# Two small moves in a decoder trunk kernel: one weight slot's high part ahead of an exponential, and a parameter transposition behind half of the query slots

## The chip, the cores and the metric

The kernel runs on one core of a Trainium2 chip. The metric is the device time of one execution in microseconds (us), as the median of three runs. TensorE is called PE here, VectorE is DVE, ScalarE is ACT, GpSimd is POOL and SyncE is SP. A line such as L725 is line 725 of the kernel file.

## What is computed

Two decoder layers over 256 tokens of width 1024, all in float32. Each layer projects the normalised tokens into queries, keys, values and two halves of a convolution module, runs windowed attention beside the convolution, projects back, and adds a feed-forward network: dense SwiGLU in layer 0, a mixture of eight experts (two per token) in layer 1.

```python
for layer in range(2):
    h = rms_norm(x, attn_norm_g[layer])
    proj = h @ w_in[layer]                      # q | k | v | conv value | conv gate
    q, k = rms_norm(q, q_norm_g[layer]), rms_norm(k, k_norm_g[layer])
    attn_out = sliding_window_attention(q, k, v, sinks[layer])
    conv_out = conformer_conv(value, gate, conv_w[layer], conv_b[layer], conv_ln_g[layer], conv_ln_b[layer])
    x = x + concat(attn_out, conv_out) @ w_out[layer]
    h = rms_norm(x, ffn_norm_g[layer])
    if layer == 0:
        x = x + (silu(h @ w_gate) * (h @ w_up)) @ w_down
    else:                                       # top 2 of 8 experts, weights from a softmax over the two
        for e in range(8):
            x = x + combine[:, e] * ((silu(h @ w_gate[e]) * (h @ w_up[e])) @ w_down[e])
```

## The kernel before

**Weight slots.** All weights stream through one sequence of slots of 128 x 2048 float32 (1 MB each). SP loads a slot into one of six `raw` buffers. ACT rounds it to `w_high` (function `high`, L725), DVE computes `w_low` = raw minus high (function `low`, L1034), and PE multiplies every tile three times: high by high, high by low, low by high (function `terms`). `w_high` and `w_low` have three buffers each, so `high(s)` waits for three things: that slot s has landed, that PE has finished slot s-3 (semaphore `w_used`), and its own place in ACT's program. `low(s)` waits for `high(s)`, and PE's function `slot(s, ...)` waits for `low(s)`. A slot of 512-column products is twelve of them for one block of 128 tokens, 24 for both blocks.

**Order.** Each engine has one program, written out by hand, and runs it strictly in that order. There is no planner: a wait in the program holds back all that stands behind it on that engine.

**The front of a layer** (function `front` of each engine) has eleven slots, called F0 to F10 here. F0 to F2 are value and gate columns of the convolution, F3 and F4 the two halves of the query weights (24 products of 512 columns each), F5 keys and values, F6 the last gate columns, F7 to F10 the output projection. In layer 0 PE also turns the convolution's parameters: 128 rows of taps for each layer and 28 rows of vectors lie in `work_b` (the taps are fetched by 16 DMAs that POOL issues, L559), and three transpositions (L1571, L1572) put them into PSUM bank 3. DVE copies them out with four instructions (L1194 to L1197, semaphore `prm_ready`). POOL's function `conv` waits for that and then builds four tiles of convolution weights with one 128 x 1024 `tensor_tensor` each (L572), the last of which also waits for the reduction L1204.

Behind F6's first half PE transposes the normalised keys (L1596) and queries (L1601). They come from DVE's chain: `low(F7)`, reduction of the keys' squares (L1207), square root on ACT, reciprocal (L1209), a 128 x 20 product with the tokens' scale (L1210), the keys (L1214), the queries (L1215). `low(F7)` is the third 128 x 2048 subtraction behind the parameters' copies, after `low(F5)` and `low(F6)`.

**The start of the experts.** The expert slots are called E0, E1, ... here (E0 is `S_MOE`). E0 and E1 are the gate weights of expert 0's first group, E2 and E3 the up weights, E4 to E7 the same for the second group. On ACT the program there is: `high(E2)`, load of the exponential's table, eight copies of gathered rows (L991), then a wait for POOL's difference of the top two logits (`zdiff_done`), the exponential of it (L995), the load of the Silu table, `high(E3)`, the Silu of the gate products (L999), `high(E4)`, `high(E5)`. The exponential's result is first read in the last expert.

Of the kernel before, what the change touches and what calls it, by code (L numbers as in the profile page):

```python
# [22 lines left out]
P = 128  # L23
# [7 lines left out]
def hybrid_trunk(nc, x, attn_norm_g, w_in, q_norm_g, k_norm_g, sinks, conv_w, conv_b, conv_ln_g,  # L31
                 conv_ln_b, w_out, ffn_norm_g, dense_w_gate, dense_w_up, dense_w_down,
                 w_router, moe_w_gate, moe_w_up, moe_w_down, out):
    _, S, D = x.shape
    L, _, IN_W = w_in.shape
    HD = q_norm_g.shape[1]
    NH = sinks.shape[1]
# [12 lines left out]
    TG = (TAPS + 3) // 4  # L50
# [19 lines left out]
    S_MOE = S_FRONT[1] + FRONT_SLOTS  # L70
# [4 lines left out]
    def at(i, per, const):  # L75

        return const if i is None else i * per + const

    with ExitStack() as ctx:
        def sb(name, shape, dt=F32):  # L80
            return ctx.enter_context(nc.sbuf_tensor(name, shape, dt))

        def sem(name):
            return ctx.enter_context(nc.semaphore(name))
# [18 lines left out]
        ident = sb("ident", [P, P])  # L103
# [59 lines left out]
        ps = ctx.enter_context(nc.psum_tensor("ps", [P, 8, 512], F32))  # L163
# [7 lines left out]
        CONST_LOADS = 16 * (3 + 4)  # L171
# [23 lines left out]
        tap_rows = work_b[:, 0:L * P].rearrange("n (l m) -> n l m", l=L)  # L195
        VEC = 3 * L * CC
        vec_rows = work_b[0:VEC + 2 * L, L * P:(L + 1) * P]
# [36 lines left out]
        consts_loaded = sem("consts_loaded")  # L234
        taps_loaded = sem("taps_loaded")
# [10 lines left out]
        prm_turned = sem("prm_turned")  # L246
# [137 lines left out]
        def head_place(h):  # L384

            return h % 2 * (NH // 2) + h // 2
# [332 lines left out]
        def _(act):  # L719
            def high(s, i=None, per=0):  # L720

                act.wait_ge(landed[s % RAW_RING], at(i, per // RAW_RING * 16, 16 * (s // RAW_RING + 1)))
                if s >= PART_RING:
                    act.wait_ge(w_used, at(i, per, s - PART_RING + 1))
                act.activation(w_part[0][:, s % PART_RING, :], raw[:, s % RAW_RING, :], ACT.Copy).then_inc(w_high_done, 1)  # L725
# [88 lines left out]
            def load_table(function):  # L814

                tables[0] += 1
                act.activation(warm[:, tables[0] - 1:tables[0]], eps_t[:, :], function)  # L817
# [173 lines left out]
                act.activation(xg[0][:, k, 0, :], first_rows(k), ACT.Copy, scale=gcols[:, GAIN[3] + k:GAIN[3] + k + 1]).then_inc(first_high_done, 1)  # L991
            act.wait_ge(first_high_done, KC)
            act.sem_inc(xg_high_done, 2)
            act.wait_ge(zdiff_done, 1)
            act.activation(zt[:, :], zt[:, :], ACT.Exp).then_inc(z_done, 1)  # L995
            load_table(ACT.Silu)
            high(S_MOE + 3)
            act.wait_ge(w_used, S_MOE + 2)
            act.activation(silu_t, ps[:, 0, :], ACT.Silu).then_inc(silu_done, 1)  # L999
            high(S_MOE + 4)  # L1000
# [20 lines left out]
        def _(dve):  # L1021
# [8 lines left out]
            def low(s, i=None, per=0):  # L1030

                dve.wait_ge(w_high_done, at(i, per, s + 1))
                r, q = s % RAW_RING, s % PART_RING
                dve.tensor_tensor(w_part[1][:, q, :], raw[:, r, :], w_part[0][:, q, :], ALU.subtract).then_inc(w_low_done, 1)  # L1034
# [22 lines left out]
            def by_row_rstd(out_, in_):  # L1057

                return dve.tensor_tensor(out_, in_, row_rstd.unsqueeze(1).to_broadcast([P, 2, S]), ALU.mult)
# [105 lines left out]
            def front(l):  # L1165
# [7 lines left out]
                def scale_val(half):  # L1173
                    dve.wait_ge(w_used, b + CHANNEL_SLOT[half, 0] + 1)
                    dve.wait_ge(rstd_copied, 2 * l + 1)
                    by_row_rstd(hpad[:, 2 * half:2 * half + 2, PAD:PAD + S], ps[:, 4 + half, :].rearrange("p (c t) -> p c t", c=2)).then_inc(val_scaled, 1)
# [5 lines left out]
                def glu(half):  # L1182
                    dve.wait_ge(val_scaled, 2 * l + half + 1)
                    dve.wait_ge(sig_done, 2 * l + half + 1)
                    dve.tensor_tensor(hpad[:, 2 * half:2 * half + 2, PAD:PAD + S], hpad[:, 2 * half:2 * half + 2, PAD:PAD + S],
                                      sig[half], ALU.mult).then_inc(glu_done, 1)
# [2 lines left out]
                scale_gate(0)  # L1189
                glu(0)  # L1190
                low(b + 4)
                if l == 0:
                    dve.wait_ge(prm_turned, 1)
                    dve.tensor_copy(taps[:, :, :, :, :].rearrange("p l i c g -> p (l i c g)"), ps[:, 3, 0:L * P]).then_inc(prm_ready, 1)  # L1194
                    dve.tensor_copy(pcol[:, :, :, :].rearrange("p v l c -> p (v l c)"), ps[:, 3, L * P:L * P + VEC]).then_inc(prm_ready, 1)
                    dve.tensor_scalar(qkg[:, 0, :], ps[:, 3, L * P + VEC:L * P + VEC + L], HD ** -0.5, None, ALU.mult).then_inc(prm_ready, 1)
                    dve.tensor_copy(qkg[:, 1, :], ps[:, 3, L * P + VEC + L:L * P + VEC + 2 * L]).then_inc(prm_ready, 1)  # L1197
                scale_val(1)
                low(b + 5)
                low(b + 6)  # L1200
                dve.wait_ge(qk_sq_done, 4 * l + 2)
# [192 lines left out]
            dve.wait_ge(ident_ready, 2)  # L1394
            dve.tensor_reduce(mask[:, :], ident[:, :].rearrange("p (j c) -> p c j", c=QUAD), AX.X, ALU.add).then_inc(prm_ready, 1)
            front(0)
            b = S_DENSE
            low(b)
# [11 lines left out]
            for f in range(DG - 1):  # L1410
# [16 lines left out]
                if f < DG - 2:  # L1427
                    low(t + 5)
            front(1)
            low(S_MOE)  # L1430
            norm_for_routing()
# [39 lines left out]
        def _(pe):  # L1471
# [3 lines left out]
            def terms(out_, tokens, tidx, weights, widx, start, stop, weights_move=True):  # L1475

                for n, (a, w) in enumerate(TERMS):
                    x_ = tokens[a][tidx]
                    w_ = weights[w][widx]
                    lhsT, rhs = (x_, w_) if weights_move else (w_, x_)  # L1480
                    last = mm(out_, lhsT, rhs, start and n == 0, stop and n == 2)
                return last

            def slot(s, k, i=None, per=0):
                pe.wait_ge(w_low_done, at(i, per, s + 1))
                return [part_slot(0, s, k), part_slot(1, s, k)]
# [65 lines left out]
            def front(l):  # L1552
                b = S_FRONT[l]
                def columns(half, m, c, ks):
                    w = slot(b + CHANNEL_SLOT[half, m], 8)
                    o = ps[:, 4 + 2 * m + half, c * S:(c + 1) * S]
                    for k in ks:
                        last = terms(o, hT, (slice(None), k, slice(None)), w, (slice(None), k, slice(c * P, (c + 1) * P)),
                                     k == 0 and c == 0, k == KC - 1, weights_move=False)
                    return last  # L1560
# [3 lines left out]
                if l == 0:  # L1564
                    spread_rstd(0)
                columns(1, 0, 1, range(KC)).then_inc(w_used, 1)
                if l == 0:
                    pe.wait_ge(consts_loaded, CONST_LOADS)
                    pe.wait_ge(taps_loaded, 16 * L * TG)
                    for m in range(L):  # L1570
                        pe.transpose(ps[:, 3, m * P:(m + 1) * P], tap_rows[:, m, :], ident[:, :])  # L1571
                    pe.transpose(ps[:, 3, L * P:L * P + VEC + 2 * L], vec_rows, ident[0:VEC + 2 * L, 0:VEC + 2 * L]).then_inc(prm_turned, 1)  # L1572

                for j in range(2):
                    w = slot(b + Q_SLOT + j, 4)
                    for k in range(4):
                        for t in range(NB):
                            last = terms(ps[:, t, :], hT, (slice(None), 4 * j + k, slice(t * P, (t + 1) * P)), w, (slice(None), k, slice(None)),
                                         j == 0 and k == 0, j == 1 and k == 3)
                    last.then_inc(w_used, 1)  # L1580

                w = slot(b + KV_SLOT, 8)
                for k in range(8):
# [22 lines left out]
                for t in range(NB):  # L1606
# [4 lines left out]
                    for h in range(NH):  # L1611

                        r, m = h % 2, head_place(h)
# [250 lines left out]
            turn_half(0, (1,))  # L1864
            turn_half(1, range(2))
            front(0)
            b = S_DENSE
            first_slots(1, b, [ps[:, 4 + m, :] for m in range(2)])
# [8 lines left out]
            pe.wait_ge(act_low_done, DG)  # L1877
            dense_down(S_FRONT[1] - 1, 0, False, True)
            front(1)
            def fill(n, bank):  # L1880

# [81 lines left out]
```

## Time and profile before

| | us |
|---|---|
| median of three runs | 1341.58 (1341.57 to 1342.34) |
| the profiled execution, device time | 1342.02 |
| its span in the trace | 1340.4 |
| PE busy in the span | 1330.5 (99%) |
| DVE busy | 1130.8 (84%) |
| ACT busy | 932.6 (70%) |

Times in the trace count from the start of the span. A row of the timeline gives start, length, engine, line, operation, output and inputs; rows with xN merge N instructions, and the bracket tells how long the engine had waited and for whom. The length of a matmul row is partly overlapped by the next matmul, so what one matmul costs is read from start to start.

### The profile page before, as it was taken

To read this page: it belongs to the slowest core of one execution; us is meant where nothing else is said; L and a number is where in the kernel's file an instruction comes from. 1 tells how busy PE (TensorE), PEld (TensorE's weight loads), DVE (VectorE), ACT (ScalarE), POOL (GpSimd) and SP (SyncE) were. 2 spreads that over 40 slices of the span, in tenths; PEclk is the share of its full clock that TensorE was granted. 3 is DMA by queue.
4 is the path that set the end of the run, shared out by engine and by line. 5 is a ranking of instruction groups with operands and counts; after the bars stand their busy time and mean duration, and the time that the engine had idled before them with its cause. 6 is when DMAs were issued, how large, how long until landed. Compare 5 with 4: busy or idle time off the path is not lost.

```text
span 1340.4 us, 16899 instructions
## 1 busy us (share of the span) xinstructions
PE 1330.5 (99%) x6957; PEld 1108.3 (83%) x6958; DVE 1130.8 (84%) x812; ACT 932.6 (70%) x787; POOL 129.5 (10%) x143
## 2 busy tenths in 40 slices
PE   9999999999999999999999999999999999999998
PEld 8879888898788888888888888888888888888886
DVE  6867666677778999998998889889888988988997
ACT  6675444465777777777777777777777777777774
POOL 3410000011046501000000000010010000000010
PEclk9999999999999999999999999999999999999999
DMA  9845566546369999999999999999999999999994
GB/s 318 251 149 191 190 190 190 188 155 195 123 219 364 393 393 392 393 360 366 395 388 373 383 393 373 368 397 390 373 380 394 372 372 395 386 355 383 395 395 177
DMA packets 199155, 430.79 MB, mean 321 GB/s; under 512 B 9768, under 2 KB 42816, under 8 KB 199072
## 3 DMA queue, kind: packets, MB, share of 16 engines
q1 hardware_dynamic: 193952, 415.40, 85.7%
q0 software_dynamic: 4576, 13.50, 2.7%
q8 instruction: 57, 0.93, 0.3%
q10 hardware_dynamic: 544, 0.75, 0.2%
q14 instruction: 26, 0.21, 0.0%
HBM read 417.56 MB, written 7.36 MB: 317 GB/s over the span
## 4 chain that ended last, share of the span: by engine, by line
PE 96%; DMA 1%; POOL 1%; DVE 1%; ACT 0%; issue 0%; SPq 0%; DVEq 0%; POOLq 0%
PE ps L1473 93%; PE ps L1766 2%; DMA raw<-in_w_in 1%; POOL work_b L559 1%; PE ps L1737 0%; PE ps L1499 0%; DMA work_b<-in_conv_w 0%; DVE h_td L1234 0%; DVE w_low L1034 0%; DVE xr L1333 0%; PE ps L1635 0%; ACT w_high L725 0%; PE ps L1601 0%; ACT cacc L810 0%; ACT L817 0%
## 5 line engine op out<-in xcount | busy, mean ns | idle before, releaser
L1034 DVE TENSOR_TENSOR w_low<-raw,w_high 128x2048 fp32r<-128x2048 f32 x387 | 893.4, 2309 | 132.8 <-ACT w_high L725 132.6
L725 ACT ACTIVATE w_high<-raw 128x2048 fp32r<-128x2048 f32 x389 | 745.2, 1916 | 268.1 <-PE ps L1473 268.0
L1473 PE MATMUL ps<-w_high,hT_both 128*128 128x512 f32 (+1 forms) x1920 | 599.3, 389 | 0.4 <-DVE w_low L1034 0.4
L1473 PEld LDWEIGHTS ps<-w_high,hT_both 128*128 128x128 f32 x1920 | 358.6, 188 | 72.4 <-DVE w_low L1034 0.8
L1473 PE MATMUL ps<-w_low,hT_both 128*128 128x512 f32 (+1 forms) x960 | 370.4, 386 | 0.0
L1473 PE MATMUL ps<-w_high,act_both 128*128 128x512 f32 x1072 | 342.4, 390 | 0.0
L1473 PEld LDWEIGHTS ps<-w_high,act_both 128*128 128x128 f32 x1072 | 201.3, 188 | 41.7 <-issue 0.3
L1473 PEld LDWEIGHTS ps<-w_low,hT_both 128*128 128x128 f32 x960 | 180.6, 188 | 34.7
L1473 PE MATMUL ps<-w_low,act_both 128*128 128x512 f32 x536 | 208.7, 389 | 0.0
L1473 PE MATMUL ps<-hT_both,w_high 128*128 128x256 f32 (+1 forms) x640 | 140.2, 338 | 0.3 <-DVE hT_both L1047 0.3
L1473 PEld LDWEIGHTS ps<-hT_both,w_high 128*128 128x128 f32 x640 | 108.9, 190 | 11.4 <-DVE hT_both L1047 0.5
L1473 PEld LDWEIGHTS ps<-w_low,act_both 128*128 128x128 f32 x536 | 100.7, 188 | 20.2
L1473 PE MATMUL ps<-hT_both,w_low 128*128 128x256 f32 x480 | 89.9, 282 | 0.0
L1473 PEld LDWEIGHTS ps<-hT_both,w_low 128*128 128x128 f32 x480 | 74.3, 191 | 3.2
L692 POOL DMA_DIRECT2D y_slots<-work_a x7 | 4.1, 593 | 711.3 <-ACT work_a L954 711.3
L934 ACT ACTIVATE work_a<-ps 128x512 f32<-128x512 f32 x55 | 33.0, 599 | 39.7 <-PE ps L1473 39.7
L1339 DVE TENSOR_TENSOR act_both<-ps,act_both 128x512 fp32r<-128x512 f32 x56 | 38.3, 684 | 0.0
L1372 DVE TENSOR_TENSOR work_a<-ps,work_a 128x512 f32<-128x512 f32 x55 | 37.6, 683 | 0.0
L916 ACT ACTIVATE act_both<-ps 128x512 fp32r<-128x512 f32 x56 | 32.5, 580 | 2.4 <-PE ps L1766 2.4
L1766 PEld LDWEIGHTS ps<-ident,work_a 128*128 128x128 f32 x224 | 27.8, 140 | 7.2
L1766 PE MATMUL ps<-ident,work_a 128*128 128x128 f32 x224 | 33.5, 272 | 0.0
L1065 DVE COPY work_a<-ps 128x512 f32<-128x512 f32 x20 | 13.8, 691 | 22.2 <-PE ps L1473 22.2
(273 smaller groups left out, 707.9 us busy)
## 6 DMA issues: line engine op xcount, KB each, us to landing
raw<-in_moe_w_gate SPq DMA_DIRECT2D x112, 1024.0 KB, 8.0
raw<-in_moe_w_up SPq DMA_DIRECT2D x112, 1024.0 KB, 7.8
raw<-in_moe_w_down SPq DMA_DIRECT2D x112, 1024.0 KB, 7.7
raw<-in_w_in SPq DMA_DIRECT2D x13, 1024.0 KB, 5.4
raw<-in_dense_w_gate SPq DMA_DIRECT2D x11, 1024.0 KB, 5.5
raw<-in_dense_w_up SPq DMA_DIRECT2D x11, 1024.0 KB, 5.5
raw<-in_dense_w_down SPq DMA_DIRECT2D x11, 1024.0 KB, 4.9
raw<-in_w_out SPq DMA_DIRECT2D x8, 1024.0 KB, 6.5
```

The source lines that it names most:

```text
L559: pool.dma_start(tap_rows[CG * i:CG * (i + 1), l, 0:QUAD * n].rearrange("g (j c) -> g j c", j=n), conv_w[l, 4 * i:4 * i + n, :].rearrange( ...
L692: pool.dma_start(y_dram[bass.ds(m * P, P), :], y_sb).then_inc(y_stored, 16)
L725: act.activation(w_part[0][:, s % PART_RING, :], raw[:, s % RAW_RING, :], ACT.Copy).then_inc(w_high_done, 1)
L916: act.activation(act_part[0][:, k % 2, :], ps[:, 2, :], ACT.Copy).then_inc(act_high_done, 1)
L934: act.activation(silu_t, ps[:, 0, :], ACT.Silu).then_inc(silu_done, 1)
L1034: dve.tensor_tensor(w_part[1][:, q, :], raw[:, r, :], w_part[0][:, q, :], ALU.subtract).then_inc(w_low_done, 1)
L1065: link(dve.tensor_copy(whole, parts[:, :, 1, :]))
L1339: dve.tensor_tensor(act_part[1][:, k % 2, :], ps[:, 2, :], act_part[0][:, k % 2, :], ALU.subtract).then_inc(act_low_done, 1)
L1372: dve.tensor_tensor(prod_t, ps[:, 1, :], silu_t, ALU.mult).then_inc(prod_done, 1)
L1473: return pe.matmul(out_, lhsT, rhs, start=start, stop=stop, skip_group_check=True)
L1766: last = pe.transpose(ps[:, 2, f * P:(f + 1) * P], prod_t[:, f * P:(f + 1) * P], ident[:, :])
```

## The change

On ACT, `high(E3)` moves ahead of the wait for POOL, the exponential and the load of the Silu table. On PE, the three transpositions of the convolution's parameters, with their two waits for DMAs, move from ahead of F3 to between F3 and F4. On DVE, the scaling of the second value half (`scale_val(1)`) moves ahead of the wait for those transpositions. No instruction is added or removed.

```diff
@@ ACT, start of the experts
             act.wait_ge(first_high_done, KC)
             act.sem_inc(xg_high_done, 2)
+            high(S_MOE + 3)
             act.wait_ge(zdiff_done, 1)
             act.activation(zt[:, :], zt[:, :], ACT.Exp).then_inc(z_done, 1)
             load_table(ACT.Silu)
-            high(S_MOE + 3)
             act.wait_ge(w_used, S_MOE + 2)
             act.activation(silu_t, ps[:, 0, :], ACT.Silu).then_inc(silu_done, 1)
             high(S_MOE + 4)
@@ DVE, front
                 low(b + 4)
+                scale_val(1)
                 if l == 0:
                     dve.wait_ge(prm_turned, 1)
                     dve.tensor_copy(taps..., ps[:, 3, 0:L * P]).then_inc(prm_ready, 1)
                     dve.tensor_copy(pcol..., ps[:, 3, L * P:L * P + VEC]).then_inc(prm_ready, 1)
                     dve.tensor_scalar(qkg[:, 0, :], ...).then_inc(prm_ready, 1)
                     dve.tensor_copy(qkg[:, 1, :], ...).then_inc(prm_ready, 1)
-                scale_val(1)
                 low(b + 5)
                 low(b + 6)
@@ PE, front
                 columns(1, 0, 1, range(KC)).then_inc(w_used, 1)
-                if l == 0:
-                    pe.wait_ge(consts_loaded, CONST_LOADS)
-                    pe.wait_ge(taps_loaded, 16 * L * TG)
-                    for m in range(L):
-                        pe.transpose(ps[:, 3, m * P:(m + 1) * P], tap_rows[:, m, :], ident[:, :])
-                    pe.transpose(ps[:, 3, L * P:L * P + VEC + 2 * L], vec_rows, ident[...]).then_inc(prm_turned, 1)
 
                 for j in range(2):
                     w = slot(b + Q_SLOT + j, 4)
...
                     last.then_inc(w_used, 1)
+                    if l == 0 and j == 0:
+                        pe.wait_ge(consts_loaded, CONST_LOADS)
+                        pe.wait_ge(taps_loaded, 16 * L * TG)
+                        for m in range(L):
+                            pe.transpose(ps[:, 3, m * P:(m + 1) * P], tap_rows[:, m, :], ident[:, :])
+                        pe.transpose(ps[:, 3, L * P:L * P + VEC + 2 * L], vec_rows, ident[...]).then_inc(prm_turned, 1)
```

## Rows read from the trace of the kernel before

**Rows 1.** The page: busy time by engine, and PE's granted clock in 40 slices.
```profile
PE 1330.5 (99%) x6957; PEld 1108.3 (83%) x6958; DVE 1130.8 (84%) x812; ACT 932.6 (70%) x787; POOL 129.5 (10%) x143
...
PEclk9999999999999999999999999999999999999999
```

**Rows 2.** Waits of PE: line, who released it, us in total, times, longest.
```profile
PE ps L1473 <- DVE w_low L1034: 0.4, 1, 0.4
...
PE ps L1571 <- DMA work_b<-in_conv_w: 0.2, 1, 0.2
```

**Rows 3.** The chain that ended last, one stretch between transpositions: start, us, what.
```profile
464.11 16.36 PE ps L1473 x72
```

**Rows 4.** Timeline of ACT at the start of the experts: start us, us, instruction.
```profile
386.44 0.20 ACT L995 ACTIVATE zt<-zt 128x2 f32<-128x2 f32 x1 [1.78 <-POOL zt L602]
386.66 1.28 ACT L817 ACT_TABLE_LOAD   x1
...
389.87 0.57 ACT L999 ACTIVATE work_a<-ps 128x512 f32<-128x512 f32 x1
390.34 3.72 ACT L725 ACTIVATE w_high<-raw 128x2048 fp32r<-128x2048 f32 x2
395.45 1.92 ACT L725 ACTIVATE w_high<-raw 128x2048 fp32r<-128x2048 f32 x1 [1.40 <-PE ps L1473]
```

**Rows 5.** Timeline of DVE and PE at the same place.
```profile
389.99 6.78 DVE L1034 TENSOR_TENSOR w_low<-raw,w_high 128x2048 fp32r<-128x2048 f32 x3 [3.32 <-ACT w_high L725]
...
386.60 0.39 PE L1473 MATMUL ps<-w_low,hT_both 128*128 128x512 f32 x1
...
391.59 0.39 PE L1473 MATMUL ps<-w_high,hT_both 128*128 128x512 f32 x1
392.34 0.50 PE L1473 MATMUL ps<-w_high,hT_both 128*128 128x512 f32 x1 [0.37 <-DVE w_low L1034]
392.68 0.40 PE L1473 MATMUL ps<-w_low,hT_both 128*128 128x512 f32 x1
```

**Rows 6.** Timeline of PE around the parameters' transpositions in layer 0.
```profile
26.73 0.28 PE L1473 MATMUL ps<-hT_both,w_low 128*128 128x256 f32 x1
26.85 0.28 PE L1473 MATMUL ps<-hT_both,w_high 128*128 128x256 f32 x1
27.36 0.41 PE L1571 MATMUL ps<-ident,work_b 128*128 128x128 f32 x2 [0.24 <-DMA work_b<-in_conv_w]
27.70 0.24 PE L1572 MATMUL ps<-ident,work_b 28*128 28x28 f32 x1
27.87 0.50 PE L1473 MATMUL ps<-w_high,hT_both 128*128 128x512 f32 x1
```

**Rows 7.** Timeline of layer 0's front: POOL, then DVE, then ACT and PE.
```profile
32.14 5.85 POOL L572 TENSOR_TENSOR gnorm<-mask,taps 128x1024 f32<-128x1024 f32 x2 [9.93 <-DVE qkg L1197]
...
34.02 3.96 POOL L572 TENSOR_TENSOR gnorm<-mask,taps 128x1024 f32<-128x1024 f32 x1
...
37.95 5.84 POOL L572 TENSOR_TENSOR h_td<-mask,taps 128x1024 f32<-128x1024 f32 x2
...
31.39 0.42 DVE L1194 COPY taps<-ps 128x256 f32<-128x256 f32 x1
...
32.54 7.59 DVE L1034 TENSOR_TENSOR w_low<-raw,w_high 128x2048 fp32r<-128x2048 f32 x2
...
42.20 3.73 DVE L1034 TENSOR_TENSOR w_low<-raw,w_high 128x2048 fp32r<-128x2048 f32 x1 [0.58 <-ACT w_high L725]
...
46.95 0.18 DVE L1210 TENSOR_TENSOR qkr<-qkr,rstd 128x20 f32<-128x20 f32 x1
...
47.84 1.22 DVE L1215 TENSOR_TENSOR work_b<-ps,qkr 128x1024 f32<-128x1024 f32 x1
...
40.26 1.91 ACT L725 ACTIVATE w_high<-raw 128x2048 fp32r<-128x2048 f32 x1
...
49.41 1.04 PE L1601 MATMUL ps<-ident,work_b 128*128 128x128 f32 x8
```

More of the change, by code:

```diff
@@ L1566, in front @@
                 columns(1, 0, 1, range(KC)).then_inc(w_used, 1)
-                if l == 0:
-                    pe.wait_ge(consts_loaded, CONST_LOADS)
-                    pe.wait_ge(taps_loaded, 16 * L * TG)
-                    for m in range(L):
-                        pe.transpose(ps[:, 3, m * P:(m + 1) * P], tap_rows[:, m, :], ident[:, :])
-                    pe.transpose(ps[:, 3, L * P:L * P + VEC + 2 * L], vec_rows, ident[0:VEC + 2 * L, 0:VEC + 2 * L]).then_inc(prm_turned, 1)
                 for j in range(2):
@@ L1580, in front @@
                     last.then_inc(w_used, 1)
+                    if l == 0 and j == 0:
[3 more added lines that the diff above has]
+                            pe.transpose(ps[:, 3, m * P:(m + 1) * P], tap_rows[:, m, :], ident[:, :])
+                        pe.transpose(ps[:, 3, L * P:L * P + VEC + 2 * L], vec_rows, ident[0:VEC + 2 * L, 0:VEC + 2 * L]).then_inc(prm_turned, 1)
                 w = slot(b + KV_SLOT, 8)
```

## The prediction

> **What bounds the kernel now.** I read the page's busy times first: PE is busy in 99% of the span, its clock in the highest tenth in every slice, so at its upper level of 2.4 GHz [rows 1]. Then the chain of waits: from the opening to the end it is PE's products almost without a break. A typical stretch is 72 products of 512 columns in 16.36 us, or 0.227 us from start to start [rows 3]. So anything that takes a hole out of PE's line, or puts one in, is paid once in full and carried unchanged to the end, since what follows is released by PE. The list of PE's waits comes next. It is short, and two of its lines are what this change is about: 0.4 us once for a low part of a weight slot, 0.2 us once for the DMA of the convolution's taps [rows 2]. Both are so small that even with both gone in full the time moves by about 0.1%. Last I read the timelines of the two places, as each move can make something else late there.
>
> **Part 1, E3's high part earlier.** Before: PE starts its last product of E2 at 391.59 and would start E3 at 391.82. It starts at 392.34, when DVE's first `low` in the row of 389.99 is done (389.99 + 2.3 = 392.3), and the second product follows after 0.34 instead of 0.23 [rows 5]. The hole costs 0.52 + 0.11 = 0.63 us. That `low` waited for ACT, and ACT for POOL (exponential at 386.44) and for the table (1.28 us) [rows 4].
>
> After: `high(E3)` needs PE to be through with E0. The second product of E1 starts at 386.60, so E0's last one at 386.15 [rows 5]. How much later ACT gets going is read from the next such release: E3's last product started at 392.68 + 10 x 0.227 = 394.95 [rows 5] and ACT started at 395.45 [rows 4], 0.50 later. So `high(E3)` starts at 386.65, not at 384.7 when ACT is free (386.44 less its 1.78 of idle time): the move gives 1.4 us (before, `low` at 389.99 less the 1.92 of `high` is 388.07), not the whole wait. It ends at 386.65 + 1.92 = 388.57. Then the exponential (0.20, POOL's value has been there since 386.44) to 388.67, the table to 389.97. Before, the Silu began 389.87 - 386.66 - 1.28 = 1.93 after the table's end; with `high(E3)` gone from between, about 0.12 is left, so Silu starts at about 390.09, and `high(E4)` 0.47 behind it (the gap 389.87 to 390.34 [rows 4]) at 390.56, against 390.34. It ends at 392.46. `low(E3)` now runs 388.6 to 390.9, a microsecond before PE wants it: that wait is gone.
>
> What is late next is E4. `low(E4)` can't start before 392.49 and ends at 394.78 (2.29, a third of 6.78 with overlaps [rows 5]). PE without the old hole wants E4 at 391.82 + 12 x 0.227 = 394.55. It starts at 394.84, and with the same slow first product it runs as if started at 394.95. Before it started E4 at 395.18. So Part 1 gives **-0.23 us** of the 0.63. Bounds: -0.63, if `high(E4)` comes 0.3 earlier than I think, and 0, if it comes 0.2 later. Who else waits: DVE's Silu product comes behind `low(E5)`, 0.2 later than before, and PE reads it only after E5, at about 400.4. E5's own `low` ends at 397.0 and PE wants it at 397.7: covered. ACT's later conversions there wait for PE (as the one of 395.45 does [rows 4]) and come earlier with it.
>
> A table load right behind a 128x2048 copy could cost more than the load: row 386.66 follows a tiny activation by 0.02 us [rows 4]. The Trainium skill's page "ScalarE: Activation LUTs", section "What ACT_TABLE_LOAD costs", states a drain of some 1.38 us on top of each switch. The row shows 0.02 us and not 1.38, in front of a short instruction; with the page's figure behind the long one, as an estimate, E4 would start 1.4 us later and Part 1 would be a loss of about 1.15 us. It is a rival below.
>
> **Part 2, the transpositions behind F3.** Before: PE's last product ahead starts at 26.85, and its neighbours are 0.12 apart, so F3 could start at 26.97. The transpositions wait for the taps until 27.36, and F3 starts at 27.87 [rows 6]. After: F3 starts at 26.97 (its low part is ready), its 24 products take 5.46, the transpositions start at 32.43, long after the taps landed, and take the same 0.51. F4 and what follows start 0.39 earlier. Bounds: 0.39, only the wait for the DMA, to 0.6, if the three follow each other more closely with their operands long there.
>
> Whether that reaches the end is decided on DVE, since the parameters now come late. The third transposition starts at 32.77 and ends at 33.01; DVE copies from 33.05. Before, the copies began at 31.39, POOL's first tile at 32.14, which is 0.75 later [rows 7]; `scale_val(1)` stood between the copies and `low(F5)`, and is now done ahead, in DVE's idle time. So `low(F5)` starts 0.55 after the first copy, at 33.60 instead of 32.54, and POOL is ready at 33.80.
>
> Then the two engines take turns. A `low` that takes 2.3 us elsewhere [rows 5] takes 3.73 here while POOL builds tiles (and two take 7.59), and a tile that takes 1.9 takes 3.96 next to a `low` [rows 7]. The ends fit one at a time: tile to 34.02, `low(F5)` from there to 36.2, tile to 37.98 (34.02 + 3.96), `low(F6)` to 40.13 (32.54 + 7.59), two tiles to 43.79 (37.95 + 5.84), `low(F7)` to 45.93 (42.20 + 3.73). Waiting for its turn, a `low` takes 2.15 after the other's end (40.13 - 37.98, 45.93 - 43.79) and a tile 1.78 (37.98 - 36.2). So I lay the same work out anew: `low(F5)` 33.60 to 35.88, tile to 37.66, `low(F6)` to 39.81, tile to 41.59. `low(F7)` needs its high part, before at 40.26 + 1.91 = 42.17, now 0.39 earlier, 41.78. POOL is first with the third tile, to 43.47, `low(F7)` to 45.61, fourth tile to **47.39**. Had DVE been first at 41.6, the fourth tile would end at the same time, so the order there doesn't matter.
>
> The reduction L1207, the root and the reciprocal take single inputs or PSUM and go on. L1210, 128x20 with both inputs in SBUF, comes 1.02 after `low(F7)`'s end (45.93 to 46.95), so at 46.6. If it has to take its turn as the large ones do, it waits for the fourth tile and ends at about 47.5 instead of 47.13. No row here shows so small an instruction waiting; the nearest are the 128x2048 ones. The Trainium skill's page "SBUF — State Buffer", section "SBUF: two separate sides", says that DVE and GpSimd share a port pair by an exclusive lock, held for the whole instruction, and that a DVE instruction with two SBUF inputs needs it against a GpSimd one that reads SBUF; it names no size. By that rule L1210 waits and the sum is the one I take; without it the part's gain would be 0.39.
>
> With L1210 0.37 later, the keys are ready at about 47.5 to 48.3, in time, and the queries (L1215, before 47.84 to 49.06) at 49.43. PE wants them 0.39 before its old 49.41 [rows 7], at 49.02. It starts at 49.48. So Part 2 gives **+0.07 us**: the wait for the taps is gone and a wait for the queries has come, of about 0.4 us. Bounds: -0.5, if the chain is in time, and +0.6, if the tiles end 0.5 later than laid out. POOL's next work behind the tiles waits for the second GLU, and PE first reads the tiles behind the scores, both well after 49.41. SP's queue is not touched: it issues the output weights independently of the parameters. DVE's `low(F8)` behind the queries moves by 0.4 with them; PE needs it only for the output projection.
>
> **Sum.** -0.23 + 0.07 = -0.16 us. Against the profiled execution (span 1340.4, device time 1342.02, which is 0.44 above the median) that is a span of 1340.2; against the median of 1341.58 it is **1341.4 us**.
>
> **Rivals.**
> (a) *Part 2 keeps its gain*: L1210 doesn't wait, or falls between two tiles. Then -0.23 - 0.39 = -0.62, with closer transpositions -0.8, so 1340.8 to 1341.0. For it: L1210 is tiny and needs only a moment of luck. Against it: the layout has POOL occupied without a break from 45.6 to 47.4.
> (b) *The queries come later still*: the place is L1215, the price is how much the fourth tile's end passes 47.4. If every turn takes the full 2.29 and 1.91 of an instruction alone, seven turns end at 33.60 + 3 x 2.29 + 4 x 1.91 = 48.1, PE waits until 50.2 and Part 2 costs 0.8; halfway, 0.4. Total +0.2 to +0.6, 1341.8 to 1342.2, slower than before. It decides from 47.3 on: each later tenth is a tenth of total time.
> (c) *E4 takes the whole gain of E3*: the table load behind the long copy is slower or `high(E4)` is later, Part 1 is 0 to +1.1 (the length of another table load, 1.28, less the 0.23 and what overlaps). Total 1341.7 to 1342.7. Against it: 0.02 us ahead of the load in rows 4.
> (d) *The move does nothing*, because `high(E3)` is held by E0 anyway: it is held, but only until 386.65 against 388.07; if that brought nothing, Part 2 alone would leave 1341.65.
> (e) *The clock*: PE's new hole near 49 us drops the clock for a stretch. At 1.2 GHz twelve products cost 2.73 more, enough for 0.2%. Against it: every slice of the page is at the upper level, with holes as large as this in it.
>
> **How the numbers follow.** Forecast 0.50, (a) 0.22, (b) 0.13, (c) 0.07, (d) 0.03, (e) 0.03, and 0.02 for something that makes it over 0.2% faster. The likeliest is 1341.4. The range goes from the best of (a), 1340.6, to the end of (b), 1342.2; as the three runs before differ by 0.8 us among themselves, I put 0.1 on each side: 1340.5 to 1342.3. 0.2% is 2.7 us, about what a measurement of this kernel can tell from no change; only (e) and the unnamed rest reach it. Faster 0.02, same 0.95, slower 0.03.
>
> **What would show it.** In the profile after: PE's waits no longer name the taps' DMA; the transpositions stand at about 32.4; POOL's first tile starts about 33.8 and its fourth ends about 47.4; L1210 takes longer than its 0.18 or starts later; PE waits before L1601 with DVE's queries as releaser. At the experts `high(E3)` starts at 386.65 less what Part 2 gave, the table load follows the exponential two microseconds later than before, E3 starts without a wait, and PE's list shows a wait of about 0.3 on `low` at E4. If E4 starts without a wait, Part 1 is nearer to 0.6. If PE doesn't wait at L1601, it is (a). A difference of microseconds would mean that something outside these two places moved, which I see no row for.

## The result, and the profile after

Thirteen runs of the changed kernel have their median at **1345.26 us** (1342.06 to 1348.29), thirteen of the kernel before at 1341.57 (1341.13 to 1342.84): a ratio of 1.0027, interval 1.0020 to 1.0034. It is slower by 3.7 us, where I had forecast 0.2 less and a range up to 1342.3. The profiled execution took 1344.20 us, with a span of 1342.6 against 1340.4. The same kernel again, later, beside other runs of before: 1347.36 against 1341.61 (ratio 1.0040, 1.0027 to 1.0053).

The page of the changed kernel, busy time and PE's granted clock, beside [rows 1]:

```profile
PE 1332.3 (99%) x6957; PEld 1108.8 (83%) x6958; DVE 1129.9 (84%) x812; ACT 933.0 (69%) x787; POOL 127.4 (9%) x143
...
PEclk9999999999999999999999999999999999999999
```

Nothing shows here: the clock stayed at its upper level, and PE is as busy as it was. PE's waits in the changed kernel (us in total, times, longest), beside [rows 2]:

```profile
PE ps L1473 <- DVE w_low L1034: 2.6, 4, 1.4
...
PE ps L1601 <- DVE work_b L1215: 0.2, 1, 0.2
```

The waits for low parts went from 0.4 us to 2.6, and the place is new. PE's four waits on `low` stand at E4 and then, tens of microseconds behind the changed code, at 416, 420 and 429 us:

```profile
394.57 0.47 PE L1473 MATMUL ps<-w_high,hT_both 128*128 128x512 f32 x1 [0.23 <-DVE w_low L1034]
...
416.39 0.50 PE L1473 MATMUL ps<-w_high,hT_both 128*128 128x512 f32 x1 [1.36 <-DVE w_low L1034]
...
419.75 0.50 PE L1473 MATMUL ps<-w_high,hT_both 128*128 128x512 f32 x1 [0.34 <-DVE w_low L1034]
...
428.95 0.50 PE L1473 MATMUL ps<-w_high,act_both 128*128 128x512 f32 x1 [0.63 <-DVE w_low L1034]
```

What this costs is read from PE's transpositions, which stand at the same places of both programs. Before, then in the changed kernel:

```profile
372.24 1.60 PE L1499 MATMUL ps<-ident,xr 128*128 128x128 f32 x12
...
1323.31 0.60 PE L1766 MATMUL ps<-ident,work_a 128*128 128x128 f32 x4
```

```profile
371.85 1.60 PE L1499 MATMUL ps<-ident,xr 128*128 128x128 f32 x12
...
1326.15 0.60 PE L1766 MATMUL ps<-ident,work_a 128*128 128x128 f32 x4
```

PE was 0.4 us ahead at 372 us and 2.8 behind at 1323, a loss of 3.2. The transpositions between them (L1766) narrow it down: the one before at 412.20 came at 411.67, the next, at 429.01, came at 431.85, and that distance of 2.84 then stays. So 3.4 us were lost between 412 and 432 us. The span is only 2.2 us longer, as 0.6 us came back behind DVE's last instruction.

One step back, ACT's waits between 390 and 440 us in the changed kernel, largest first, with one line left out:

```profile
ACT w_high L725 <- DMA raw<-in_moe_w_gate: 5.5, 3, 3.9
ACT w_high L725 <- DMA raw<-in_moe_w_up: 2.9, 4, 1.4
...
ACT w_high L725 <- DMA raw<-in_moe_w_down: 1.9, 1, 1.9
```

Before, ACT had no wait on a load in that stretch; its conversions waited for PE alone. So the weights come late. How late, from issue to landing (us), for the ten or eleven slots that SP issued between 393 and 424 us, the kernel before and then the changed one:

```profile
DMA to landing us min/median/max: 7.9/11.3/11.7
```

```profile
DMA to landing us min/median/max: 11.2/15.1/16.4
```

Before, ACT wanted slots E10 to E13 at 406.80, 409.74, 412.46 and 415.67 us, and SP issued them at 394.6, 396.8, 399.7 and 402.4. That gives a load 12 to 13 us. Those of 11.5 just make it, with a margin of about 1 us; those of 15 to 16 don't. From 430 to 1300 us the traffic is at 383 GB/s in both kernels, 2.7 us for a slot of 1 MB, against PE's 2.8 us: what is late catches up slowly. For loads issued between 424 and 470 us the median landing is still 11.4 us against 9.9; from 560 us on it is the same. What filled the stretch in between is seen in windows of 4 us (busy time of PE, PEld, DVE, ACT, POOL; clock; DMA share; GB/s), before and then after:

```profile
396.00:400.00 4.00, 4.00 (x20) 3.30 (x19) 3.67 (x3) 3.20 (x2) 1.61 (x1) 1.00 1.03 371
```

```profile
396.00:400.00 4.00, 4.00 (x19) 3.31 (x18) 3.83 (x4) 2.29 (x2) 1.46 (x1) 1.00 0.91 39
400.00:404.00 4.00, 4.00 (x22) 3.29 (x21) 2.82 (x3) 3.26 (x4) 0.00 (x0) 1.00 0.70 154
```

39 GB/s instead of 371, with the DMA engines nine tenths busy. One window exaggerates, as E9's load was issued 1.7 us earlier in the changed kernel: over the 20 us from 392 to 412 it is 174 GB/s instead of 261. What the DMA engines were busy with in the changed kernel from 396 to 400 us:

```profile
DMA packets 77, 0.16 MB, mean 39 GB/s; under 512 B 0, under 2 KB 0, under 8 KB 77
...
q1 hardware_dynamic: 77, 0.16, 91.4%
```

These are packets of the weight loads alone, 77 of them in 4 us; the window 412 to 416 has 809. So the loads' own packets stood. What else is between issue and landing there is POOL's token list: four indirect writes (L613), one token number of 4 bytes to each place, out of an SBUF tile into a table in DRAM. That they are the reason isn't in these rows; e4 below shows it. POOL's rows, before and then after:

```profile
388.59 0.19 POOL L609 CAST list_i<-row_f 128x4 int32<-128x4 f32 x1
389.39 1.10 POOL L613 DMA_INDIRECT slot_tokens<-tok_i,list_i  x1 [0.61 <-POOL list_i L609]
390.80 2.34 POOL L613 DMA_INDIRECT slot_tokens<-tok_i,list_i  x1 [0.30 <-issue]
...
405.78 0.61 POOL L616 DMA_DIRECT2D slot_tok<-slot_tokens  x1 [8.18 <-DMA slot_tokens<-tok_i,list_i]
```

```profile
388.21 0.19 POOL L609 CAST list_i<-row_f 128x4 int32<-128x4 f32 x1
389.01 2.50 POOL L613 DMA_INDIRECT slot_tokens<-tok_i,list_i  x1 [0.61 <-POOL list_i L609]
391.82 0.98 POOL L613 DMA_INDIRECT slot_tokens<-tok_i,list_i  x1 [0.30 <-issue]
...
410.15 0.61 POOL L616 DMA_DIRECT2D slot_tok<-slot_tokens  x1 [12.69 <-DMA slot_tokens<-tok_i,list_i]
```

The first write takes 2.50 us where it took 1.10, and the list is complete 4.4 us later. Beside that write stands DVE's `low(E3)`, which the change put there, and which stood at 389.99 before [rows 5]:

```profile
388.24 2.31 DVE L1034 TENSOR_TENSOR w_low<-raw,w_high 128x2048 fp32r<-128x2048 f32 x1 [1.93 <-ACT w_high L725]
```

It ends at 390.55; the write that started at 389.01 ends 0.96 later, at 391.51, nearly the 1.10 of the first write before. It stood still until DVE was through. Before, the same `low(E3)` had met the second write instead: 2.34 us from 390.80, its end 0.86 us behind `low(E3)`'s. The change moved the meeting from the second write to the first.

### The profile page after: what moved, and what is told of

It reads as the page before. It is cut to its first block, busy times and chain, and to the rows that moved or that the text cites. A ratio compares the mean times of both kernels' runs of the same rounds, so it can differ in the third digit from the quotient of the medians.

```text
span 1342.6 us, 16899 instructions
## 1 busy us (share of the span) xinstructions
PE 1332.3 (99%) x6957; PEld 1108.8 (83%) x6958; DVE 1129.9 (84%) x812; ACT 933.0 (69%) x787; POOL 127.4 (9%) x143
## 4 chain that ended last, share of the span: by engine, by line
PE 95%; DVE 2%; DMA 2%; ACT 1%; issue 0%; SPq 0%; DVEq 0%; ACTq 0%
PE ps L1473 92%; PE ps L1766 2%; DMA raw<-in_moe_w_down 1%; DVE w_low L1034 1%; ACT w_high L725 1%; PE ps L1737 0%; PE ps L1499 0%; DMA xr<-in_x 0%; DVE h_td L1234 0%; DVE xr L1333 0%; PE ps L1635 0%; PE ps L1601 0%; ACT cacc L810 0%; DVE work_b L1215 0%; PE ps L1858 0%
## 5 line engine op out<-in xcount | busy, mean ns | idle before, releaser
L1766 PEld LDWEIGHTS ps<-ident,work_a 128*128 128x128 f32 x224 | 27.9, 140 | 7.2
L1766 PE MATMUL ps<-ident,work_a 128*128 128x128 f32 x224 | 33.5, 272 | 0.0
L572 POOL TENSOR_TENSOR gnorm<-mask,taps 128x1024 f32<-128x1024 f32 x4 | 13.6, 3421 | 208.9 <-DVE w_low L1034 197.4
```

Of the source, the lines that this page charges most:

```text
L572: pool.tensor_tensor(wconv[c], mask[:, :].unsqueeze(1).unsqueeze(1).to_broadcast([P, TG, 4, QUAD]), taps[:, l, :, c, :].unsqueeze(3).to_br ...
L1766: last = pe.transpose(ps[:, 2, f * P:(f + 1) * P], prod_t[:, f * P:(f + 1) * P], ident[:, :])
```

## Experiments

Two theories stood at the start. **The load** (theory A of the expectations): the early `low(E3)` frees a `raw` buffer earlier, so SP issues E9 at 390.57 instead of 392.31 and that load itself collides with the writes. **The shift** (theory B): Part 2 starts the expert stage 0.4 us earlier. A third came only after e1 to e4. **The port** (theory C): the early `low(E3)` holds the port that DVE and POOL share, so the token list's writes leave later and fall among the weight loads. The table load had been my rival (c).

All medians stand beside runs of the kernel before on the same chip: 1341.92 for e1 to e4, 1341.89 for e5 to e8, 1341.61 for v1, v2 and a0. The ratio counts all runs and not only the medians.

**One part alone.** e1 has only ACT's part:

```diff
+            high(S_MOE + 3)
             act.wait_ge(zdiff_done, 1)
             act.activation(zt[:, :], zt[:, :], ACT.Exp).then_inc(z_done, 1)
             load_table(ACT.Silu)
-            high(S_MOE + 3)
```

> Part 1 alone (E3's high part ahead of the exponential; parameters turned as before). Theory A, the early load: with low(E3) done 1.4 us earlier, SP issues the load of slot E9 that much earlier, in the middle of POOL's four indirect writes of the token list, and the loads of E10 to E14 then land some 5 us later; PE waits for them around 412 to 430. Then this kernel alone has the whole loss: 3 to 5 us over before (1344.5 to 1346.5), a wide spread, and loads of E10 to E13 that take 13 to 16 us from issue to landing instead of 8 to 12. Theory B, the shift: it is the whole expert stage's starting 0.4 us earlier (Part 2) that brings the loads and the token writes into each other's way; then this kernel is 0.2 us faster than before, 1341.3, as was worked out for Part 1.

Measured: 1343.55 us, ratio 1.0023 (1.0014 to 1.0033). The eleven runs fall into two groups, six from 1342.80 to 1343.55 and five from 1346.01 to 1348.17; their mean is 2.8 us above that of the kernel before. In the profiled one (1342.88) it is the cast that DVE's instruction met:

```profile
388.19 2.34 POOL L609 CAST list_i<-row_f 128x4 int32<-128x4 f32 x1
390.83 1.10 POOL L613 DMA_INDIRECT slot_tokens<-tok_i,list_i  x1 [0.30 <-POOL list_i L609]
```

DVE's `low(E3)` started at 388.20, 0.01 us behind the cast's row, and a cast of 512 numbers took 2.34 us instead of 0.19. So two outcomes are seen: `low(E3)` gets in ahead of the cast, or behind it and ahead of the write.

e2 has only PE's and DVE's part, the transpositions behind F3:

```diff
                     last.then_inc(w_used, 1)
+                    if l == 0 and j == 0:
+                        pe.wait_ge(consts_loaded, CONST_LOADS)
...
```

> Part 2 alone (parameters turned behind the first query slot; exponential and table load as before). Theory A: no loss, PE is 0.35 us ahead from 50 us to the end as in the profile of the changed kernel, so 1341.2, with before's narrow spread. Theory B: the loss of 3 to 5 us is here.

Measured: 1341.79 us, ratio 0.9996 (0.9987 to 1.0006). The loss is ACT's part alone. Its loads landed after 12.7 us (median), and ACT waited for seven of them, 4.4 us in all, yet PE waited for no `low` but E3's: behind ACT's margin there is some more.

**The load held.** The changed kernel, with E9's load bound to PE's release of E2:

```diff
                 if s >= RAW_RING:
                     sp.wait_ge(w_low_done, at(i, per, s - RAW_RING + 1))
+                if i is None and s == S_MOE + 9:
+                    sp.wait_ge(w_used, S_MOE + 3)
```

> The whole change, with one wait added on SP: the load of E9 is issued only when PE is through with E2 (about 392.0), which is where it stood before (392.3). Low(E3) stays early. Theory A: the loss is gone, 1340.9 to 1341.3, faster than before by what both parts gave at 400 us (0.5 us), and E10 lands about 8 us after issue. A rival within it, that the loss comes from DVE, ACT or PE being early rather than from this one load: 1344 to 1346 as the changed kernel. A second rival, that only luck decides in which order the queues serve loads and token writes: a spread as wide as the changed kernel's, with a median between.

Measured: 1343.13 us, ratio 1.0005 (0.9996 to 1.0014). The cast took 2.34 us here too, so the first write ended even later than in the changed kernel, and the same slots landed 13.0 us after their issue (median). By the median 1.2 us of loss are left, though the interval reaches no loss, and no run is above 1344.70. The gain that I expected did not come, but the interval lies wholly below the changed kernel's (1.0020 to 1.0034): holding one load took most of the loss away. So the load's moment matters. That it is the whole cause is refuted by e8 below.

**No list.** The changed kernel without the four indirect writes and the wait for them. It leaves out the token list, so experts 1 to 6 work on token 0's rows; all loads and products are there.

```diff
                 pool.wait_ge(list_cleared, 16)
-                for b in range(NB):
-                    for r in range(2):
-                        pool.indirect_dma_start(out=slot_dram[:, :], ...).then_inc(tokens_listed, 16)
-                pool.wait_ge(tokens_listed, 16 * 2 * NB)
```

> The whole change, without POOL's four indirect writes of the token list into memory and the wait for them (so every expert but the first and last gets the cleared list's token 0 in all rows; all other work is done). Theory A, in which load and token writes have to meet: no loss, 1340.7 to 1341.1, loads of E10 to E13 in 5 to 11 us. If the loads are late for a reason of their own (too little lead over PE at the memory's rate): 1343 to 1346 even so.

Measured: 1342.17 us, ratio 1.0001 (0.9992 to 1.0010). The loss is gone, and so are ACT's waits on loads. The loads of 393 to 424 us:

```profile
DMA to landing us min/median/max: 5.1/7.1/7.5
```

7.1 us instead of 15.1, and instead of the 11.3 of the kernel before. So the writes cost the loads 4 us in the kernel before as well, hidden there by the margin. The cast took 2.34 us here too: held without writes behind it, it costs nothing. The gain of 0.8 to 1.2 us that I expected did not come in the median.

**The start of low(E3) as before.** The changed kernel, but DVE waits for the Silu first:

```diff
             first_low()
+            dve.wait_ge(silu_done, DG + 1)
             low(S_MOE + 3)
```

> The whole change, but DVE holds low(E3) until ACT's Silu is done (about 390.35, before it ran from 389.99); high(E3) stays early. Theory C, the shared port: in the changed kernel low(E3) starts within hundredths of a microsecond of POOL's cast of the token list (388.2) and blocks either the cast (2.34 us instead of 0.19) or the first of four indirect writes (2.50 instead of 1.10), so that the token writes come 1 to 2 us later, among the weight loads instead of ahead of them, and the loads land late. Then here POOL's cast takes 0.19 and its first indirect write 1.1, E10 lands 8 to 9 us after issue, the runs have before's narrow spread, and the price is only PE's own wait for the held low, 1.1 us: 1341.9 to 1342.4. Rival, that any run with both parts in it has the late loads because PE and ACT are early: 1344 to 1346 here too.

Measured: 1342.41 us, ratio 1.0006 (0.9997 to 1.0015). First write 1.10 us at 389.22; the only wait on `low` is the 1.1 us at E3 that this edit makes. ACT's move is harmless when DVE does not follow it. The wait also put E9's load back, to 392.83, so this run doesn't tell the port from the load.

**Only just behind the cast.** The changed kernel, `low(E3)` bound to PE's release of E1, which is about a microsecond later:

```diff
             first_low()
+            dve.wait_ge(w_used, S_MOE + 2)
             low(S_MOE + 3)
```

> The whole change, but DVE holds low(E3) until PE is through with E1 (about 389.0): late enough for POOL's cast to be done always, early enough for PE to find E3 ready at 391.5. Theory C: the cast takes 0.19 in every run, so the two groups of times seen with Part 1 alone (1342.8 to 1343.6 and 1346.0 to 1348.2) become one. If the first indirect write is the one that is blocked, as in the changed kernel's profile (2.50 us), that is the slow group: 1344.5 to 1347. If it gets in ahead of low(E3) and takes 1.1, the loads are in time: 1341.0 to 1341.5. Rival, that the spread is chance in the DMA queues and not a race at the port: two groups here as well.

Measured: 1342.30 us, ratio 1.0006 (0.9997 to 1.0015), but from 1341.63 to 1346.95, as wide as e1, where I had expected one group. The profiled run is the slowest of them:

```profile
388.50 0.19 POOL L609 CAST list_i<-row_f 128x4 int32<-128x4 f32 x1
389.30 3.17 POOL L613 DMA_INDIRECT slot_tokens<-tok_i,list_i  x1 [0.61 <-POOL list_i L609]
```

`low(E3)` started at 389.21, 0.09 us ahead of the write. The edit had moved the meeting from the cast to the write. Across these kernels a start within a tenth of a microsecond of another's was won by either side. That one kernel's executions differ in it would explain the two groups of e1 and the spread here; of each kernel only one execution was profiled, or two, so it isn't shown.

**Only the writes late.** The changed kernel with the writes behind `low(E3)`. The expectation speaks of the cast too; it stands ahead of the wait and wasn't held.

```diff
                 pool.wait_ge(list_cleared, 16)
+                pool.wait_ge(w_low_done, S_MOE + 4)
                 for b in range(NB):
```

> The whole change, but POOL's placement of the list (and so the cast and all four indirect writes) waits for low(E3) to be done, about 390.6. Theory C: POOL's work then comes as late as or later than in the run in which low(E3) won the port (cast done 390.5), cast takes 0.2 unless the next low catches it; one group of times, near or above the lower group of Part 1 alone, 1342.8 to 1344.5, the more the later the writes are. If it was the coincidence alone that cost, and not that the writes come later: 1340.9 to 1341.3.

Measured: 1343.33 us, ratio 1.0008 (0.9999 to 1.0017), as expected by the median, though runs go down to 1341.05 and the interval reaches no loss. Loads 13.6 us. The first write ended at 392.91, 1.4 us later than in the changed kernel, and the loss is smaller: later isn't always worse.

**The kernel before, with late writes.** This has neither part of the change, only a wait of 2 us ahead of the writes:

```diff
                 pool.wait_ge(list_cleared, 16)
+                pool.wait_ge(silu_done, DG + 1)
                 for b in range(NB):
```

> The kernel before (neither part), with one wait added: POOL's placement of the list waits for ACT's Silu (390.44), so that the four indirect writes come some 2.5 us later than before; low(E3) and the load of E9 stay as they were. Theory C in its form that lateness of the writes among the loads is the cost: loads of E10 to E13 land in 13 us and more instead of 8 to 11.5, and the time is 1 to 4 us over before (1343 to 1346). If what matters is only low(E3) or E9's load being early: no loss, 1341.6 to 1342.1.

Measured: 1345.46 us, ratio 1.0027 (1.0015 to 1.0039). The first write, and PE's waits:

```profile
391.25 1.93 POOL L614 DMA_INDIRECT slot_tokens<-tok_i,list_i  x1 [2.56 <-ACT work_a L1000]
```

```profile
PE ps L1474 <- DVE w_low L1035: 2.4, 4, 1.3
```

Four waits of 2.4 us in all, against 2.6 in the changed kernel, and the same ratio. Late writes alone, with `low(E3)` and E9's load where they were, can make a loss of the whole size.

**No exponential.** In both of these kernels the second weight is Silu(z)/z instead of e^z/(1+e^z), which is the same number, so the Silu table is loaded once and early. v1 also lets POOL write the list first and form the logit difference behind it; v2 keeps POOL's order.

```diff
-            load_table(ACT.Exp)
+            load_table(ACT.Silu)
...
             high(S_MOE + 3)
-            act.wait_ge(zdiff_done, 1)
-            act.activation(zt[:, :], zt[:, :], ACT.Exp).then_inc(z_done, 1)
-            load_table(ACT.Silu)
```

> The whole change, with the exponential taken out of the way: the second expert weight exp(z)/(1+exp(z)) is the sigmoid of z, here silu(z)/z, so ACT needs no exponential, no table load between E2 and E4 and no wait for POOL, and POOL can place the token list and issue its indirect writes first and the logit difference behind them. If lateness of the writes among the weight loads is the cost (shown by the kernel before with held writes), the writes, 2 us earlier than in the kernel before, give loads in 6 to 10 us, PE waits neither at E3 nor at E4, and the time is 0.36 (Part 2) + 0.63 (all of E3's hole) under before: 1340.7 to 1341.2, with a narrow spread. If the loads suffer from the writes wherever these are: 1343 and more.

> The same without an exponential, but with POOL's order as in the changed kernel (logit difference first, writes behind it). Low(E3) then still starts at about 388.2, next to POOL's cast: the loss of the changed kernel is back although ACT is faster, 1343 to 1347 in one or two groups. If ACT's exponential and table load had been what costs: 1340.7 to 1341.2 as the kernel above.

Measured: v1 1341.64 us, ratio 1.0000 (0.9992 to 1.0009); v2 1345.36 us, ratio 1.0031 (1.0019 to 1.0043). Both have `high(E3)` early and no switch of tables at E3. In v1 the first write is at 386.96, ahead of `low(E3)`, loads land after 11.0 us, and neither E3 nor E4 waits. In v2 `low(E3)` came at 389.25 and met the instruction ahead of the cast:

```profile
389.30 2.29 POOL L593 TENSOR_TENSOR row_f<-place_b 128x4 f32<-128x4 f32 x1
391.66 0.19 POOL L610 CAST list_i<-row_f 128x4 int32<-128x4 f32 x1
392.47 3.18 POOL L614 DMA_INDIRECT slot_tokens<-tok_i,list_i  x1 [0.62 <-POOL list_i L610]
```

So the table is not the cost; where the list stands to `low(E3)` is. v1's E9 load is as early as in the changed kernel (390.48), and there is no loss: an early load alone doesn't make one either. v1 takes the loss away, but my forecasts for it, loads in 6 to 10 us and a gain of 0.4 to 0.9 us, failed in the landing and in the median. Its interval goes from 0.9992 to 1.0009, and I call it no improvement.

> The changed kernel itself, beside the others on the same chip. As before: 1342 to 1348, median near 1345. In the profile either the cast or the first indirect write is blocked by low(E3).

Measured: 1347.36 us, as told at the top, with the first write at 390.78 taking 2.50 us again.

**All in one table.** POOL's row of places (`row_f`, the last step ahead of the cast) is the start; the time from it to the end of the first write says whether DVE was in the way. Undisturbed it is 2.2 us. The stretch is PE's time from the transposition at 372 us to the one at 1323, of which the kernel before took 951.07 us; it leaves out what two openings differ by.

| kernel | row_f to end of first write | loads land, median | stretch over before | median over before |
|---|---|---|---|---|
| before | 2.2 | 11.3 | | |
| e2, Part 2 alone | 2.2 | 12.7 | +0.04 | -0.1 |
| e5, low held | 2.2 | 12.9 | +0.79 | +0.5 |
| v1, list first | 2.2 | 11.0 | -0.66 | 0.0 |
| changed | 3.6 | 15.1 | +3.22 | +3.7 |
| the same again | 3.6 | 16.6 | +5.11 | +5.8 |
| e3, load held | 4.0 | 13.0 | +0.88 | +1.2 |
| e1, Part 1 alone | 4.0 | 13.2 | +1.18 | +1.6 |
| e6, just behind | 4.2 | 16.1 | +5.06 | +0.4 |
| e7, writes held | 4.6 | 13.6 | +1.22 | +1.4 |
| e8, before, writes held | 5.0 | 15.0 | +3.11 | +3.6 |
| v2, no exponential | 6.4 | 15.0 | +3.25 | +3.8 |

Of the profiled executions those with 2.2 are at most 0.8 us over before, and e5's 0.8 holds its own wait of 1.1; every other is 0.9 to 5.1 over. How much a late list costs isn't a function of how late it is: e7 and e8 differ by 0.4 us in the first write and by 1.9 in the stretch. In the changed kernel only the first write ends later (391.51 against 390.49); the fourth, at 395.56 + 1.90 = 397.46, ends no later than before (395.71 + 1.89 = 397.60). It must also matter which loads stand in the queues at that moment, as e3 says of E9's. I have no view that shows how.

## Why the prediction was wrong

**The bound** was read rightly: PE's line, every hole in it paid once. The 3.4 us lost between 412 and 432 us are carried unchanged to 1323.

**Part 1, locally, held.** `high(E3)` ran from 386.29, the table load stood two microseconds later, E3 started without a wait, and PE waited at E4 for 0.23 us (forecast about 0.3). From E3's last product at 393.96 the hole at E4 is 0.38, with 0.08 in the product behind it, 0.46 us in place of the old 0.63: a gain of 0.17 against my 0.23. ACT's rows at the place, beside [rows 4]:

```profile
386.29 1.92 ACT L725 ACTIVATE w_high<-raw 128x2048 fp32r<-128x2048 f32 x1 [2.00 <-PE ps L1473]
388.11 0.19 ACT L996 ACTIVATE zt<-zt 128x2 f32<-128x2 f32 x1
388.31 1.28 ACT L817 ACT_TABLE_LOAD   x1
...
389.72 0.58 ACT L999 ACTIVATE work_a<-ps 128x512 f32<-128x512 f32 x1
```

Rival (c) fell: the load of the table stands 0.01 us behind the exponential. The drain of 1.38 us of the Trainium skill's page "ScalarE: Activation LUTs", section "What ACT_TABLE_LOAD costs", is not seen here, neither behind a long copy nor anywhere in these rows.

**Part 2 held.** The changed kernel's front, DVE, POOL and PE:

```profile
32.71 0.42 DVE L1195 COPY taps<-ps 128x256 f32<-128x256 f32 x1 [0.95 <-PE ps L1580]
...
46.29 0.79 DVE L1210 TENSOR_TENSOR qkr<-qkr,rstd 128x20 f32<-128x20 f32 x1
...
41.21 5.83 POOL L572 TENSOR_TENSOR h_td<-mask,taps 128x1024 f32<-128x1024 f32 x2
...
49.06 1.09 PE L1601 MATMUL ps<-ident,work_b 128*128 128x128 f32 x8 [0.19 <-DVE work_b L1215]
```

This execution's opening is 0.32 us ahead of the other's (PE's product ahead of F3 at 26.53 instead of 26.85). With that taken off, the copies were forecast for 32.73 and came at 32.71, the fourth tile's end for 47.07 and came at 47.04. L1210, 128x20, took 0.79 us instead of 0.18 [rows 7]: it stood behind POOL's tile and ended 0.04 behind it. PE came to L1601 22.53 us behind that product, before 22.56: -0.03, where I had said +0.07. Its wait for the queries was 0.2 us, where I had said 0.4. The gain was eaten as described, and e2's -0.1 agrees within its interval.

**What failed** is the paragraph "Who else waits" of Part 1. It follows `low(E3)` down PE's and ACT's lines and never asks who else is on DVE's port at 388 us, nor what SP issues once `low(E3)` has freed its `raw` buffer. In Part 2 I had laid out DVE's and POOL's turns instruction by instruction; at the experts I moved a DVE instruction of 2.3 us with two SBUF inputs by 1.8 us and did not look at POOL at all. Its cast stood at 388.59 and its first write at 389.39, in the gap of DVE that `low(E3)` moved into, and the second write's 2.34 us beside the first's 1.10 already showed a hold. The layout of Part 2 applied there would have given a cast ending with `low(E3)` at about 390.9, or a write ending a microsecond later.

The second half of the failure is the last sentence, that no row pointed outside the two places. There was one: the landing time of the loads. I took "ahead of need" for granted as ACT never waited for a load. 11.3 us of landing against the 12 to 13 until use is a margin of one microsecond, and the edit moved traffic within it: the loads came to 15.1, and PE lost 3.4 us where the sum had nothing. So the loss wasn't a term of the wrong size but one that was missing from the sum, and the rivals, all within the two places, had none of it.

The range had a slip too: its lower end takes 1340.6 for the best of (a), where (a) itself ends at 1340.8. It changes nothing here.

**The local gains were real.** e4 and v1, without the late loads, are not faster than before by their medians. Over the stretch of the table they are: by 0.22 us in e4, where my sum for Part 1 was 0.23, and by 0.66 in v1, where the whole hole at E3 was 0.63. One execution of each was profiled. The medians hide gains of this size: PE came to the transposition at 372 us between 371.80 and 373.63 in these executions.

**What stays open.** Why writes of 4 bytes hold the weight packets so, and why a first write ending 1 us later does so more. How the changed kernel's loss divides between that write and E9's early load: e8 makes it by the writes alone, e3 takes most of it away by the load alone, and e7, with both a late list and an early load (390.96), has only 1.2 us of it.

## What to carry to other kernels

When an instruction moves, list what runs on *every* engine in the stretch that it moves into, not only what depends on it. Here a DVE instruction with two inputs in SBUF delayed a cast of 0.19 us, and an indirect write, until it was through itself. And of every prefetch read two numbers ahead of any edit near it, from issue to landing and from issue to use: where they are a microsecond apart, moving small transfers by a microsecond can be a change on the critical path. If one kernel's runs spread over several microseconds more than its neighbour's, look for two instructions that start within a tenth of each other. And to judge a small edit from two traces, measure between two places that both share, behind the opening.

## What the runs showed of the hardware

The lock between DVE and POOL holds for very small instructions: 0.19 us became 2.34 for a 128x4 cast, 0.18 became 0.79 for a 128x20 product, both ending as the other engine's instruction did. An indirect DMA issued by POOL is held as well, 1.10 us becoming 2.50 to 3.18, beside an ordinary float32 subtraction; it ends 0.86 to 0.97 us behind it. The Trainium skill's page "SBUF — State Buffer", section "SBUF: two separate sides", has the rule for two SBUF inputs against a GpSimd instruction that reads SBUF, and these rows agree with it; its warning on blocked descriptors is for DVE's 2-port modes. Whether the DMA's descriptors waited here or its reading of the list in SBUF, no run tells.

Four indirect writes of 128 entries of 4 bytes each held up the weight loads around them. Without them the loads land after 7.1 us, with them after 11.3 in the kernel before and 15.1 in the changed one, where 77 packets of the loads kept the DMA engines nine tenths busy for 4 us at 39 GB/s. When the writes run counts about as much as that they run.
